# Expert slots without a token are left out of the row transfers, and the experts' rows are stored by index

## The reference, cut to what matters

```python
A = T * TOP_K                                   # 1024 * 2 = 2048
padded = (counts + MOE_BLOCK - 1) // MOE_BLOCK * MOE_BLOCK
...
slot_tok = jnp.full((P,), T, jnp.int32).at[dest].set(st)
...
xb = x_pad[slot_tok].reshape(NB, MOE_BLOCK, D)

def expert_block(args):
    xblk, e = args
    hdn = jax.nn.silu(xblk @ w_gate[e]) * (xblk @ w_up[e])
    return hdn @ w_down[e]

yb = lax.map(expert_block, (xb, block_expert)).reshape(P, D)
y = jax.ops.segment_sum(yb.astype(jnp.float32) * slot_w[:, None], slot_tok, num_segments=T + 1)[:T]
```

## Time and profile before

| | us |
|---|---|
| median of 3 runs | 3064.89 |
| lowest, highest run | 3061.75, 3072.95 |
| the profiled execution, its own time | 3062.8 |
| its span, first to last instruction | 3061.0 |
| TensorE busy in the span | 2804.0 (92%) |
| VectorE busy | 1772.7 (58%) |
| ScalarE busy | 1325.6 (43%) |
| GpSimd busy | 448.9 (15%) |
| bytes moved by DMA | 418.81 MB |
| of these, issued by GpSimd (queue q0) | 33.03 MB |
| of these, issued by ScalarE (queue q10) | 20.97 MB |

### The profile page before, as it was taken

The page is one execution under the profiler, slowest core; times in us unless marked ns, Lnnn a source line. Parts: engine busy times, 40 slices in busy tenths (PEclk is TensorE's granted clock), DMA queues, the critical chain, the costliest instruction groups (busy, mean ns, idle before and its releaser), DMA issues. The chain is left out here.

```text
span 3061.0 us, 39291 instructions
## 1 busy us (share of the span) xinstructions
PE 2804.0 (92%) x14800; PEld 2321.0 (76%) x14801; DVE 1772.7 (58%) x2286; ACT 1325.6 (43%) x1879; POOL 448.9 (15%) x397
## 2 busy tenths in 40 slices
PE   8999798988969599999995898879899999998999
PEld 7988577777758588888884876657688888887887
DVE  4441267777754599899985833856564343433313
ACT  5111255555532278777774432344453232322212
POOL 0000056445620200000001500310000000000000
PEclk9999899999979699999997999999899999999999
DMA  6545200011025399999994411000141111110114
GB/s 213 186 162 217 106 28 35 35 36 51 15 103 212 124 369 410 408 408 411 408 404 159 153 44 28 1 2 1 46 136 48 48 48 48 48 48 24 49 50 153
DMA packets 159576, 418.81 MB, mean 137 GB/s; under 512 B 21164, under 2 KB 101088, under 8 KB 146144
## 3 DMA queue, kind: packets, MB, share of 16 engines
q1 hardware_dynamic: 144848, 363.15, 31.9%
q0 software_dynamic: 8848, 33.03, 2.8%
q10 hardware_dynamic: 5760, 20.97, 1.7%
HBM read 348.44 MB, written 68.69 MB: 136 GB/s over the span
## 5 line engine op out<-in xcount | busy, mean ns | idle before, releaser
L3383 DVE SCALAR_TENSOR_TENSOR ffn_up_acc<-psum,ffn_up_taps,ffn_up_acc 128x1023 f32<-128x1023 f32 x88 | 112.8, 1282 | 285.4 <-ACT ffn_up_acc L3304 279.6
L136 PE MATMUL psum<-part,ffn_up_w_low 128*128 128x512 f32 x704 | 277.3, 394 | 0.0
L135 PE MATMUL psum<-low,ffn_up_w_high 128*128 128x512 f32 x704 | 276.0, 392 | 0.0
L134 PE MATMUL psum<-part,ffn_up_w_high 128*128 128x512 f32 x704 | 273.4, 388 | 0.7 <-DVE low L3369 0.7
L134 PE MATMUL psum<-part,expert_x_high 128*128 128x512 f32 x512 | 204.7, 400 | 2.9 <-issue 1.5
L136 PE MATMUL psum<-part,expert_x_low 128*128 128x512 f32 x512 | 201.0, 393 | 0.0
L134 PE MATMUL psum<-project_w_high,high 128*128 128x448 f32 (+1 forms) x512 | 194.7, 380 | 3.5 <-DVE low L387 3.5
L3304 ACT ACTIVATE ffn_up_acc<-psum,ffn_up_taps 128x1024 f32<-128x1024 f32 x44 | 53.1, 1207 | 333.9 <-PE psum L136 333.9
L136 PE MATMUL psum<-project_w_high,low 128*128 128x448 f32 (+1 forms) x512 | 193.7, 378 | 0.0
L135 PE MATMUL psum<-project_w_low,high 128*128 128x448 f32 (+1 forms) x512 | 193.7, 378 | 0.0
L129 DVE TENSOR_TENSOR expert_down_low<-expert_down,expert_down_high 128x2048 fp32r<-128x2048 f32 x64 | 143.8, 2288 | 47.3 <-ACT expert_down_high L124 47.3
(11 more groups left out here) (581 smaller groups left out, 6948.3 us busy)
## 6 DMA issues: line engine op xcount, KB each, us to landing
expert_gate<-in_w_gate_dram SPq DMA_DIRECT2D x32, 2048.0 KB, 10.0
expert_up<-in_w_up_dram SPq DMA_DIRECT2D x32, 2048.0 KB, 10.2
expert_down<-in_w_down_dram SPq DMA_DIRECT2D x32, 2048.0 KB, 10.9
ffn_up_w<-in_ffn_w_up_dram SPq DMA_DIRECT2D x44, 512.0 KB, 3.7
y_rows<-expert_y ACTq DMA_DIRECT2D x32, 512.0 KB
ffn_down_w<-in_ffn_w_down_dram SPq DMA_DIRECT2D x39, 256.0 KB, 2.5
project_w<-in_w_in_dram SPq DMA_DIRECT2D x4, 2048.0 KB, 12.2
ret_feat<-project_out SPq DMA_DIRECT2D x4, 2048.0 KB, 10.4
```

Of the source, the lines that this page charges most:

```text
L134: pe.matmul(out, left[0], right[0], start=start, stop=False)
L135: pe.matmul(out, left[0], right[1], start=False, stop=False)
L136: return pe.matmul(out, left[1], right[0], start=False, stop=stop)
L3383: v.scalar_tensor_tensor(out=acc[c][u][:, i:], in0=wide(psum, 4 * u + 2 * c, 2)[:, 0:S - i], scalar=taps[:, last_tap - i, ds(at, 1)], in1= ...
```

## The change

Empty slots get a row number that lies outside the tensors. `row_no` starts each token's number at minus 4096, and after the matmuls 4096 is added back: a filled slot then holds c * 1024 + token for choice c, an empty one holds 4096. `slot_to` is this number, `slot_from` the token alone.

```diff
-            pool.wait_ge(zeroed, 1)
-            pool.wait_ge(product, (RW_BLOCKS + 1) * TT)
-            pool.dma_start(idle_rows.rearrange("(b p) d -> p b d", p=P),
-                           per_block(zeros[:], idle_rows.shape[0] // P)).then_inc(cleared, 16)
...
-            sp.wait_ge(cleared, 16)
...
-            link(v.scalar_tensor_tensor(out=where[:], in0=block_at[:], scalar=float(SLOT_BLOCK), in1=pos[:], op0=ALU.mult, op1=ALU.add))
-            v.tensor_copy(slot_index[:], where[:])
...
             v.wait_ge(ids_made, 1)
-            link(v.tensor_copy(ids[:], bank[0][:, 0:SLOT_BLOCKS]))
+            link(v.tensor_scalar(to_row[:], bank[0][:, 0:SLOT_BLOCKS], float(NO_ROW), None, ALU.add))
+            v.tensor_copy(slot_to[:], to_row[:])
+            link(v.tensor_scalar(from_row[:], to_row[:], float(S), -float(S), ALU.is_ge, ALU.mult))
+            link(v.tensor_tensor(from_row[:], from_row[:], to_row[:], ALU.add))
+            v.tensor_copy(slot_from[:], from_row[:])
             weigh(1)
...
-            act.wait_ge(y_ready, n * 2 + 2)
-            act.dma_start(y_rows[ds(n * P, P), :], y[:]).then_inc(stored, 16)
...
+                pool.tensor_copy(pick[u][:], slot_from[:, at]).then_inc(picked[u], 1)
                 pool.wait_ge(picked[u], per_u + 1)
                 pool.sem_inc(passed, 1)
                 pool.indirect_dma_start(out=rows_in[u][:], out_offset=None, in_=h_rows,
-                                        in_offset=bass.IndirectOffsetOnAxis(ap=pick[u][:, 0:1], axis=0)).then_inc(gathered[u], 16)
+                                        in_offset=bass.IndirectOffsetOnAxis(ap=pick[u][:, 0:1], axis=0),
+                                        bounds_check=S - 1, oob_is_err=False).then_inc(gathered[u], 16)
+
+            def store(at, n):
+
+                if not isinstance(n, int) or n:
+                    pool.wait_ge(stored, n * 16)
+                    pool.sem_inc(passed, 1)
+                pool.tensor_copy(put[:], slot_to[:, at]).then_inc(put_ready, 1)
+                pool.wait_ge(put_ready, n + 1)
+                pool.wait_ge(y_ready, n * 2 + 2)
+                pool.sem_inc(passed, 1)
+                pool.indirect_dma_start(out=y_rows, out_offset=bass.IndirectOffsetOnAxis(ap=put[:, 0:1], axis=0), in_=y[:], in_offset=None,
+                                        bounds_check=2 * S - 1, oob_is_err=False).then_inc(stored, 16)
...
+            for u in range(2):
+                pool.memset(rows_in[u][:], 0.0).then_inc(rows_cleared, 1)
+            pool.wait_ge(rows_cleared, 2)
             for u in range(2):
                 fetch(slice(u, u + 1), u, 0)
-            with pool.Fori(1, half) as j:
+
+            def serve(j, u, first):
+
+                n = j * 2 + u
+                pool.wait_ge(x_turned, n - 1)
+                pool.wait_ge(gathered[u], j * 16)
+                fetch(ds(n, 1), u, j)
+                if not first:
+                    store(ds(n - 3, 1), n - 3)
+
+            serve(1, 0, True)
+            serve(1, 1, False)
+            with pool.Fori(2, half) as j:
                 for u in range(2):
-                    pool.wait_ge(x_turned, j * 2 + u - 1)
-                    pool.wait_ge(gathered[u], j * 16)
-                    fetch(ds(j * 2 + u, 1), u, j)
+                    serve(j, u, False)
+            for n in range(EXPERTS - 3, EXPERTS):
+                store(slice(n, n + 1), n)
...
             def gather(t):
                 for c in range(2):
-                    pool.indirect_dma_start(out=got[t % 2][:, c, :], out_offset=None, in_=y_rows,
-                                            in_offset=bass.IndirectOffsetOnAxis(ap=slot_index[:, c, t:t + 1], axis=0))\
-                        .then_inc(gathered[t % 2], 16)
+                    pool.dma_start(got[t % 2][:, c, :], y_rows[c * S + t * P:c * S + (t + 1) * P, :]).then_inc(gathered[t % 2], 16)
```

More of the change, by code:

```diff
@@ L146, in project_stage @@
 def project_stage(nc, bank, ident, x_dram, ident_dram, gain_dram, squares, feat, low, w_dram, mu_dram, rw_raw, rw_dram, ret_dram,
-                  idle_rows, cn):
+                  cn):
     PIECES = 4
@@ L179, in project_stage @@
         mu_loaded, prev_loaded, shift_order, shifted = (st.sem(n) for n in ("mu_loaded", "prev_loaded", "shift_order", "shifted"))
-        zeroed, cleared, raw_stored, row_zeroed = (st.sem(n) for n in ("zeroed", "cleared", "raw_stored", "row_zeroed"))
+        zeroed, raw_stored, row_zeroed = (st.sem(n) for n in ("zeroed", "raw_stored", "row_zeroed"))
         block = st.open()
@@ L1407, with route_stage @@
 FAR = 1e30
-def route_stage(nc, bank, ident, a, out_w, parts, rest, x, mixed, h_rows, ids, slot_weight, slot_index, more, weights):
+NO_ROW = 4 * S
+def route_stage(nc, bank, ident, a, out_w, parts, rest, x, mixed, h_rows, slot_from, slot_to, slot_weight, more, weights):
     w_plain, w_low, w_high = out_w
@@ L1449, in route_stage @@
         blocks, first, last_of = (st.sb(n, [P, EXPERTS]) for n in ("blocks", "first", "last_of"))
-        own, place, full, far, at_far, pos, start, block_at, where = (
-            st.sb(n, [P, 2, TT]) for n in ("own", "place", "full", "far", "at_far", "pos", "start", "block_at", "where"))
+        own, place, full, far, at_far, pos, start, block_at = (
+            st.sb(n, [P, 2, TT]) for n in ("own", "place", "full", "far", "at_far", "pos", "start", "block_at"))
         past = st.sb("past", [P, 2, HALF, FULL_STEPS])
@@ L1853, in load_down, with expert_stage @@
         sp.dma_start(flat(self.down[u][:]), self.of("w_down", e)).then_inc(self.down_loaded[u], 16)
-def expert_stage(nc, bank, ident, a, w, part, more, ids, h_rows, y_rows):
+def expert_stage(nc, bank, ident, a, w, part, more, slot_from, slot_to, h_rows, y_rows):
     with Stage(nc, "expert") as st:
@@ L1864, in expert_stage @@
         pick = [st.sb(f"pick{u}", [P, 1], I32) for u in range(2)]
+        put = st.sb("put", [P, 1], I32)
         rows_in = [st.sb(f"rows_in{u}", [P, D]) for u in range(2)]
@@ L2052, in fetch @@
             def fetch(at, u, per_u):
-                pool.tensor_copy(pick[u][:], ids[:, at]).then_inc(picked[u], 1)
+                pool.tensor_copy(pick[u][:], slot_from[:, at]).then_inc(picked[u], 1)
                 pool.wait_ge(picked[u], per_u + 1)
@@ L3680, in program, with mixers2 @@
                     w = ExpertWeights(nc, weights, a)
-                    route_stage(nc, bank, ident, a, w.out_w, parts, w.beyond, x, mixed, h_rows, ids, slot_weight, slot_index, more, w)
-                    expert_stage(nc, bank, ident, a, w, part, more, ids, h_rows, y_rows)
-                mixers2(nc, a, psum, bank, ident, feat, part, x, y_rows, slot_index, slot_weight, x2_dram)
+                    route_stage(nc, bank, ident, a, w.out_w, parts, w.beyond, x, mixed, h_rows, slot_from, slot_to, slot_weight, more, w)
+                    expert_stage(nc, bank, ident, a, w, part, more, slot_from, slot_to, h_rows, y_rows)
+                mixers2(nc, a, psum, bank, ident, feat, part, x, y_rows, slot_weight, x2_dram)
         second_half(nc, a, out, psum, bank, ident, feat, part, squares, x2_dram)
-def mixers2(nc, a, psum, bank, ident, feat, part, x, y_rows, slot_index, slot_weight, x2_dram):
+def mixers2(nc, a, psum, bank, ident, feat, part, x, y_rows, slot_weight, x2_dram):
     with ExitStack() as ctx:
```

27 lines of the change are left out of this document (14 added, 13 removed).

## The result

After takes 3072.56 us (median of 20 runs, 3067.43 to 3079.95) against 3063.78 us before (20 runs, 3053.38 to 3072.95). The ratio is 1.0031, with a 95% interval of 1.0022 to 1.0040. That is 8.8 us by the medians, inside the 0.5% that counts as the same, and 0.6 us from the forecast of 3072. The sum behind the forecast was +7.65. So the number came out, and the question is whether its terms did.

A forecast was written before the change was run, and what follows sets the result against it. The prediction took TensorE to bound the expert loop, so saved bytes gain nothing; terms 0.8 + 5.2 - 0.55 + 2.2 + 0 = +7.65 us on 3064.9 gave 3072.5, rounded to 3072, range 3058 to 3086.

The forecast's parts named there:

- Bound by TensorE, bytes without a buyer: Expert loop: TensorE sets the 17.98 us period, so the bytes saved on gathers and stores gain nothing.
- The cleared blocks, 0: GpSimd's transfer at 222.8 us, which the change removes, runs beside a busy TensorE; taking it away gives 0 us.
- In the loop: 0 us.: Loop over the experts: fewer bytes per block leave the period at 17.98 us, a change of 0 us.
- Routing's end, +0.8: End of the routing: four more small VectorE instructions at 0.2 us each, +0.8 us (0.6 to 1.0).
- The first gather, +5.2: Start of the expert stage: two clears push the first fetch beside VectorE's subtractions, +5.2 us; +2.9 if the copy slips in.
- The last blocks, -0.55: End of the expert stage: without the store's issue, ScalarE's split of the last down weights starts earlier, -0.55 us.
- The last store, +2.2: End of the expert stage: GpSimd's indirect store lands later than ScalarE's plain one, +2.2 us (0.5 to 2.5).
- The fetch behind, 0: Start of the next stage: the plain fetch of got moves the same bytes behind the same traffic, 0 us (-1.5 to +1).
- (a): Rival: the ends cost little, the copy slips in, store and fetch are quick; +2.0 to +4, near 3068; chance 0.14.
- (b): Rival: the DMA engines pace the loop, so fewer bytes save 1.3 us a block; near 3035; chance 0.06.
- (c): Rival: the scatter store lands late under load and holds ScalarE in the loop; near 3108; chance 0.10.
- (d): Rival: nothing is left out, queue q0's bytes stay, and the time is the forecast's; chance 0.05.

The follow-up runs named there:

- e6: After without the clears, every empty slot's gather index clamped to the last row so that all rows are gathered; 18.12 us a block.
- e10: After with two unused tiles that give weights, x and hidden tiles one remainder by 256 bytes; 3062.54 us, ratio to before 0.9999.
- e11: The kernel of e8 measured once more, word for word, beside e10; 3056.92 us, ratio to before 0.9967.
- e2: Before with two unused tiles that put the expert stage's tiles at after's addresses, no instruction changed; 3063.99 us, ratio to before 0.9999.
- e4: After without the clears, the first two blocks' empty-slot indices clamped to the last row; ratio to before 1.0018.
- e8: Before with two unused tiles that give all operands of gate, up and lower one remainder by 256 bytes; 3052.65 us, ratio 0.9973.
- e7: After with the next stage's first tile of got fetched by SyncE instead of GpSimd; ratio to before 1.0017.
- e9: After without clears, aligned, first tile of got fetched by SyncE, its norm work ahead of the weights' splits; 3058.1 us, ratio to before 0.9991.
- e5: Before with only the gathers leaving empty slots out, clearing included; stores and the later gather as in before; ratio to before 1.0008.

## Why the prediction was right, and where it was not

**Bound by TensorE, bytes without a buyer.** Right, and shown twice: e6 gathers all rows again at no cost in the loop, e10 has e11's period.

**The cleared blocks, 0.** Right: the first stage ends between 359.6 and 362.5 us in the six kernels that have the transfer, and between 359.9 and 362.8 in the seven that don't.

**"In the loop: 0 us."** The step that failed. From TensorE's first turn to the start of the second copy of the last block but one, after takes 580.87 us and before 575.69: +5.18. e2 has +4.95 of it from the addresses alone; 0.2 us stay unassigned. The prediction read the distance of the matmuls, 0.230 and 0.229 us, as a floor that only a wait could lift. It was 231 ns of a range from 227 to 234. Nothing in the rows of before could tell that; the list of tiles in the diff could have told that they move.

**Routing's end, +0.8.** +0.62, at the lower bound.

**The first gather, +5.2.** +3.03, by the case that was named as the lower bound with +2.9. The copy slipped in before VectorE (0.19 us at 1062.04; VectorE's subtractions start at 1062.15), and only the gather was stretched, to 2.35 us. The two clears took 1.84 us together, as priced. That the copy would wait for the second clear's report, my reason for the upper value, is not seen: 0.07 us lie between them. e4 shows that the clears are all of the term.

A gather beside a VectorE instruction with two inputs is stretched here too: 2.35 us; in e4, where it had started 0.8 us ahead of that instruction, it took 1.27. The prediction read this as speaking against the Trainium skill, "SBUF — State Buffer", section "Who interferes with whom", by which the writing of descriptors is inferred not to be held. After has the rows that tell, from GpSimd's plain fetches in the next stage:

```profile
1696.60 1.10 POOL L2309 DMA_DIRECT2D got<-y_rows  x2
...
1696.00 1.22 DVE L2551 TENSOR_TENSOR weighed<-h,project_end_gain 128x1024 f32<-128x1024 f32 x1
1697.14 1.02 DVE L129 TENSOR_TENSOR project_w_tm_low<-project_w_tm,project_w_tm_high 128x832 fp32r<-128x832 f32 x1
```

Two plain issues beside such instructions take 0.55 us each, as the four at 1674.22 with VectorE idle do. So the trace agrees with the page, and the reading in the prediction was wrong: only indirect issues are stretched. They have `pick`, a tile in SBUF, as an operand; that reading it is what is held fits the page's rule, but no run tests it.

**The last blocks, -0.55.** Right. ScalarE's split now starts 0.49 us behind the copy's start (1649.66 to 1650.15) where it was 1.07, and TensorE's wait behind it is 7.77 us in all six kernels with ScalarE's store and 7.18 in all seven with GpSimd's: -0.59. In after:

```profile
1657.23 0.79 PE L134 MATMUL psum<-expert_down_high,expert_hidden_high 128*128 128x512 f32 x1 [7.18 <-DVE expert_hidden_low L129]
```

The distance of the last two copies, 15.91 us before and 15.46 after, doesn't show it: the same kernel has 16.09 and 15.27 there (e8 and e11).

**The last store, +2.2.** +3.30, beyond the bound of 2.5, and most of it is not the landing that the term priced. The rows of the stage's end: ScalarE's first instruction behind its wait for the store and its drain, the last thing that an engine does before the barrier; in after GpSimd's drain too. Before, then after (duration in ns, start in us):

```profile
L2007 ACTq TENSOR_LOAD <-more x1: 474/474/474, 1656.9 to 1656.9; - x1
L89 ACTq DRAIN  x1: 8/8/8, 1657.8 to 1657.8; - x1
```

```profile
L2006 ACTq TENSOR_LOAD <-more x1: 469/469/469, 1669.8 to 1669.8; - x1
L89 ACTq DRAIN  x1: 8/8/8, 1670.7 to 1670.7; - x1
L89 POOLq DRAIN  x1: 5526/5526/5526, 1667.3 to 1667.3; - x1
```

ScalarE is released 4.06 us behind the copy's end and not 2.69: +1.37. Of this 0.82 is the later start of the issue; from issue to release the indirect store of a half-filled block is 0.55 us slower than the plain one (3.21 against 2.66), not 1.7, and nearer to the 0.4 that the prediction set aside. Then everyone waits for GpSimd, whose drain ends at 1672.84, 2.1 us behind ScalarE's: a wait that was in no term. In before GpSimd's drain, 9.3 us long, lay at 1581.3, far ahead of the stage's end. The remaining -0.2 us is a first fetch that starts sooner behind the barrier. All seven kernels with GpSimd's stores have this drain, 5.5 us long and ending 7.13 us behind the copy's end. It ends 3.4 us behind the store's last packet (1669.42); why so late is open, and no run moves the last store alone to another engine.

**The fetch behind, 0.** Column e fell by 1.51, the lower bound exactly, and column f took 0.90 of it back; e7 and e9 show that column f gives back what e gains. Net -0.6, about as much as e + f varies by in one kernel (115.23 us in e8, 114.65 in e11).

**Not in the sum.** The convolution loop of the next stage went from 22.39 to 22.18 us a round in every kernel whose routed tiles moved, and stayed at 22.40 in e5, where they did not. Five rounds are -1.1 us, a placement effect of the other sign; by e2 it comes from addresses alone, but which operands make it was not looked for.

Together: 0.62 + 3.03 + 4.73 + 3.30 - 1.51 + 0.90 = 11.07, less 2.03 us behind the first convolution, half of it variation, is 9.04; the spans differ by that once the 3.16 us ahead are taken off. That the forecast's sum was near is luck, since errors cancelled: +5.3 in column c (4.73 where it had -0.55) and +1.1 for the store stood against -0.2 for the routing, -2.2 for the gather and -2.6 for what lies behind the first fetch.

**The rivals.** (a) holds for the gather and for the store's landing, not for the stage's end. (b) falls by e6. (c) falls: GpSimd waits for the stores 130.5 us in 27 times, at most 6.7, and ScalarE, which has 16 us until it needs `y` again, has no wait for a store in the list. From the waits of after in 1100 to 1600 us:

```profile
POOL y_rows L2069 <- ACT expert_y L1969: 188.4, 28, 18.7
POOL expert_put L2065 <- DMA y_rows<-expert_y,expert_put: 130.5, 27, 6.7
```

(d) falls by q0.

## What to carry to other kernels

Before asking what a change does to bytes, list the tiles it adds, drops or resizes: every tile allocated behind them moves, and where TensorE is the bound a moved operand can cost or give more than the change itself. Give stationary and moving operands the same remainder by 256 bytes, and compare two kernels only at equal places. Where an engine that was idle at a stage's end gets the last transfer, its own drain can be the last to reach the barrier: here 2.1 us behind the engine that waited for the landing. And a transfer that is taken off full DMA engines, or brought forward, is worth only what the engine that sets the end can use.

## What the hardware showed that I had not expected

Matmuls of 128x128 by 128x512 followed each other at 227 to 234 ns at a full clock, with no wait, next to no DMA and no other engine at work, and the time followed the distance of their two operands' SBUF addresses modulo 256 bytes: least at a distance of 0, then at +64, and most at the six others, all in steps of 32 bytes. In this kernel, between the places of after and the aligned ones, that is 0.40 us in a block of 18 and some 0.3% of the whole time. Why +64 is better than -64 is open, as are steps under 32 bytes and other shapes than 512 columns.

GpSimd's plain DMA issues took 0.55 us each beside a VectorE instruction with two inputs as well as alone; indirect ones went from 1.05 us to 2.35.
